# Softmax probabilities of a streaming encoder's cross-attention as fp16 halves, turned round by a DMA transpose instead of by TensorE

## The reference, cut to what matters

```
q = x_q.reshape(b, t, MEM_HEADS, MEM_HEAD_DIM)                       # 4 heads of 64
s = jnp.einsum('bthd,bmhd->bhtm', q, mem_k).astype(jnp.float32) * (MEM_HEAD_DIM ** -0.5)
p = jax.nn.softmax(s, axis=-1).astype(mem_v.dtype)                   # over 256 memory tokens
o = jnp.einsum('bhtm,bmhd->bthd', p, mem_v).reshape(b, t, GROUP_W)
y_x = o * jax.nn.silu(x_g)
```

## Time and profile before

| | us |
|---|---|
| three timed runs | 1544.96, 1550.85, 1550.87 (median 1550.85) |
| profiled execution, own time | 1546.23 |
| its span, first to last instruction | 1544.4 |
| busy: PE / DVE / ACT / POOL | 1482.1 / 1122.6 / 533.2 / 241.4 |
| mean granted TensorE clock | 0.986 |

### The profile page before, as it was taken

The page is one execution under the profiler, slowest core; times in us unless marked ns, Lnnn a source line. Parts: engine busy times, 40 slices in busy tenths (PEclk is TensorE's granted clock), DMA queues, the critical chain, the costliest instruction groups (busy, mean ns, idle before and its releaser), DMA issues.

```text
span 1544.4 us, 32608 instructions
## 1 busy us (share of the span) xinstructions
PE 1482.1 (96%) x12014; PEld 1291.5 (84%) x12014; DVE 1122.6 (73%) x3012; ACT 533.2 (35%) x1093; POOL 241.4 (16%) x188
## 2 busy tenths in 40 slices
PE   5877999999999999999999999999999999999976
PEld 4766888888888898888888888888889888888864
DVE  7996675949587685949677694958767694958754
ACT  7773232332233332323323232323323233233332
POOL 2252110111111111111111011111110011111100
PEclk9988999999999999999999999999999999999988
DMA  9884607154442706354451615354260625444136
GB/s 270 237 300 131 225 18 231 79 163 163 163 163 61 251 28 193 120 163 163 131 195 34 236 58 178 146 163 163 93 233 14 216 97 163 163 150 171 43 113 239
DMA packets 148771, 236.19 MB, mean 153 GB/s; under 512 B 71945, under 2 KB 97725, under 8 KB 148733
## 3 DMA queue, kind: packets, MB, share of 16 engines
q1 hardware_dynamic: 148733, 235.69, 45.4%
HBM read 193.62 MB, written 26.05 MB: 142 GB/s over the span
## 4 chain that ended last, share of the span: by engine, by line
PE 86%; DVE 8%; DMA 2%; ACT 1%; issue 1%; SPq 1%; DVEq 0%; ACTq 0%
PE u L431 19%; PE u L432 19%; PE u L433 19%; PE sps L431 4%; PE sps L433 4%; PE sps L432 4%; PE qps L431 3%; PE qps L433 3%; PE qps L432 3%; DVE z L1177 3%; PE qps L507 2%; DVE w_hl L1159 2%; PE ops L431 1%; PE ops L432 1%; PE ops L433 1%
## 5 line engine op out<-in xcount | busy, mean ns | idle before, releaser
L431 PE MATMUL u<-h_hi,w_hl 128*128 128x256 f16 (+1 forms) x2992 | 789.6, 270 | 4.5 <-issue 1.9
L432 PE MATMUL u<-h_lo,w_hl 128*128 128x256 f16 (+1 forms) x2992 | 788.7, 269 | 0.0
L433 PE MATMUL u<-h_hi,w_hl 128*128 128x256 f16 (+1 forms) x2992 | 788.6, 269 | 0.0
L1177 DVE SCALAR_TENSOR_TENSOR z<-glu,cst,z 128x256 f32<-128x256 f32 (+1 forms) x1020 | 432.8, 494 | 0.5
L431 PEld LDWEIGHTS u<-h_hi,w_hl 128*128 128x128 f16 x2992 | 293.8, 99 | 47.8 <-issue 7.9
L433 PEld LDWEIGHTS u<-h_hi,w_hl 128*128 128x128 f16 x2992 | 293.6, 99 | 32.6
L432 PEld LDWEIGHTS u<-h_lo,w_hl 128*128 128x128 f16 x2992 | 293.7, 99 | 31.4
L734 ACT ACTIVATE gate<-u,inv 128x256 f32<-128x256 f32 (+1 forms) x204 | 83.7, 462 | 244.4 <-PE u L433 242.6
L1517 DVE TENSOR_TENSOR ob<-sps,ob 128x512 f32<-128x512 f32 (+1 forms) x33 | 21.3, 686 | 132.8 <-PE sps L433 132.8
L431 PE MATMUL sps<-ring,y_hi 128*128 128x512 f32 (+1 forms) x280 | 111.6, 398 | 3.2 <-DVE y_lo L1214 2.5
L431 PE MATMUL qps<-ring,y_hi 128*128 128x512 f32 (+1 forms) x264 | 106.2, 402 | 8.3 <-DMA ring<-wo_split 8.3
(11 more groups left out here) (195 smaller groups left out, 2011.0 us busy)
## 6 DMA issues: line engine op xcount, KB each, us to landing
ring<-wo_split SPq DMA_DIRECT2D x264, 512.0 KB, 6.5
ob<-in_x_prompt SPq DMA_DIRECT2D x34, 512.0 KB, 3.7
out<-ob SPq DMA_DIRECT2D x32, 512.0 KB, 3.1
xb<-in_x_prompt SPq DMA_DIRECT2D x30, 512.0 KB, 4.9
w_hl<-in_w_in SPq DMA_DIRECT2D x20, 512.0 KB, 7.4
wo_split<-ring SPq DMA_DIRECT2D x16, 512.0 KB, 3.9
rows<-in_w_out SPq DMA_DIRECT2D x16, 256.0 KB, 4.9
ob<-in_mem_prompt SPq DMA_DIRECT2D x2, 512.0 KB, 6.5
```

Of the source, the lines that this page charges most:

```text
L431: nc.tensor.matmul(out, a_hi, b_hi, start=first, stop=False)
L432: nc.tensor.matmul(out, a_hi, b_lo, start=False, stop=False)
L433: return nc.tensor.matmul(out, a_lo, b_hi, start=False, stop=last)
L1177: ins = nc.vector.scalar_tensor_tensor(z[:, c, 0:n], glu[:, c, k:k + n], w, z[:, c, 0:n], ALU.mult, ALU.add)
```

## The change

- The probabilities of a pair are no longer transposed on PE. ACT writes the high half straight from `probs`, multiplied by the reciprocal, as fp16 into the row-major buffer `prow`; DVE writes the remainder (`probs_lo`: probs times reciprocal minus the high half). `softmax_norm` shrinks to `softmax_rcp`, two small instructions; the probabilities carry a factor of 2^14.
- SP then issues one DMA transpose of both tiles and both halves of the pair (`probs_across`, 128 x 2048 fp16), behind ring piece 6 (pair 0) and piece 7 (pair 1), whose loads move from the chunk's start to this place.
- `prow` is one buffer for both pairs, so `probs_hi` of a pair waits until the transpose of the pair before has landed.
- The values become fp16 halves with one scale for all, a power of two from their sum of squares (`value_squares` on ACT, `value_sum` on PE, `value_scale` on DVE); `yx_out` multiplies by the inverse. `attend` is still 12 matmuls of 256 columns with 128-column stationaries, in fp16.
- The second tile of the next rows goes into `xp`, the memory of `probs`, not into `xb`. In chunk 0 the wait for `row_lo` moves from before the ninth ring piece to behind the sixteenth.
- The cached values and keys for the sample are loaded earlier, into `probs`, and their handling has other places in the lists.

```
-            sp.dma_start ... xb[:, :], x_next  (q == RING - 1, after the wait for row_lo)
@@ SP, sync_chunk
                 if first:
+                    for p in range(PAIRS):
+                        sp.wait_ge(p_lo_ok.sem, (p + 1) * nt)
+                        probs_across(p, n)
+                    sp.dma_start(xp, x_next).then_inc(x_in[1].sem, 16)
                     sp.wait_ge(wlo_ok.sem, FT)
...
-                        sp.wait_ge(o_piece.sem, o_piece.at(i, q - RING + 1))
+                        if not first and RING - PAIRS <= q < RING:
+                            sp.wait_ge(p_lo_ok.sem, p_lo_ok.at(i, (q - RING + PAIRS + 1) * nt))
+                        else:
+                            sp.wait_ge(o_piece.sem, o_piece.at(i, q - RING + 1))
                         sp.dma_start(ring[:, q % RING].bitcast(F32), wo_split[q]).then_inc(wo_in[q % RING].sem, 16)
+                        if not first and RING - PAIRS <= q < RING:
+                            probs_across(q - RING + PAIRS, n)
...
-                    if q == RING and rows_m:
-                        if x_next is None:
+                    if q == (PIECES - 1 if first else RING) and rows_m:
+                        if first or x_next is None:
                             sp.wait_ge(row_lo_ok.sem, row_lo_ok.at(i, 1))
                         row_across(0, rows_m[0])
@@ PE, attend
-                        ins = three(ops[:, p * N:p * N + n], v_hi[:, k, p, v], v_lo[:, k, p, v],
-                                    pt_hi[:, h, k, 0:n], pt_lo[:, h, k, 0:n], ...
+                pe.wait_ge(pt_in[p].sem, pt_in[p].at(i, 16))
+                products = [(va, pa, k, h) for h in range(2) for k in range(MT) for va, pa in ((0, 0), (0, 1), (1, 0))]
+                for step, (va, pa, k, h) in enumerate(products):
+                    ins = nc.tensor.matmul(ops[:, p * N:p * N + n].rearrange("d (t m) -> d t m", t=nt),
+                                           v16[:, va, k, p, h * HD:h * HD + P], pt16[:, p, 0:nt, pa, h, k, 0:m], ...
@@ ACT, probs_hi
+                act.wait_ge(rcp_ok.sem, rcp_ok.at(i, 2 * p + 2))
+                if n == N and needed(pt_in[1 - p].at(i, 16 * p)):
+                    act.wait_ge(pt_in[1 - p].sem, pt_in[1 - p].at(i, 16 * p))
+                for t, t0, m in tiles(n):
+                    for h in range(2):
+                        ins = nc.scalar.activation(prow[0:m, s % 2, 0, h, :], probs[0:m, s % 2, h, :], ACT.Copy,
+                                                   scale=rcp[0:m, s, h:h + 1])
@@ DVE, probs_lo
+                        ins = nc.vector.scalar_tensor_tensor(prow[0:m, s % 2, 1, h, :], probs[0:m, s % 2, h, :],
+                                                             rcp[0:m, s, h:h + 1], prow[0:m, s % 2, 0, h, :],
+                                                             ALU.mult, ALU.subtract)
@@ PE, chunk
                 project(i, n, "a_x")
-                probs_t(i, n, 0)
                 scores(i, n, 1)
                 project(i, n, "a_b")
                 attend(i, n, 0)
                 project(i, n, "a_g")
-                probs_t(i, n, 1)
                 mix(i, n)
                 project(i, n, "b_g")
                 attend(i, n, 1)
@@ DVE, chunk
-                softmax_norm(i, n, 0)
+                softmax_rcp(i, n, 0)
-                taps(i, n, 12, 15)
+                taps(i, n, 12, 14)
+                probs_lo(i, n, 0)
+                taps(i, n, 14, 15)
```

More of the change, by code:

```diff
@@ L493, in scores @@
                 ins.then_inc(s_ready.sem, 1)
[L495 to L509, removed]
             def attend(i, n, p):
@@ L516, in attend, with value_sum @@
                         pe.wait_ge(v_l.sem, 1)
[L517 to L520, removed]
[L521 to L524 removed]
+                    if type(i) is int and i == CHUNKS:
+                        pe.wait_ge(v_l.sem, 2)
+                pe.wait_ge(pt_in[p].sem, pt_in[p].at(i, 16))
+                nt, m = len(tiles(n)), min(n, P)
+                products = [(va, pa, k, h) for h in range(2) for k in range(MT) for va, pa in ((0, 0), (0, 1), (1, 0))]
+                for step, (va, pa, k, h) in enumerate(products):
+                    ins = nc.tensor.matmul(ops[:, p * N:p * N + n].rearrange("d (t m) -> d t m", t=nt),
+                                           v16[:, va, k, p, h * HD:h * HD + P], pt16[:, p, 0:nt, pa, h, k, 0:m],
+                                           start=step == 0, stop=step == len(products) - 1)
+                ins.then_inc(pv_ready.sem, 1)
+            def value_sum(k):
+                pe.wait_ge(vsq_ok.sem, k + 1)
+                if k == 0:
+                    pe.wait_ge(mn_lo.sem, 4)
+                    bank = qps[:, 0, 0:2]
+                else:
+                    pe.wait_ge(yx_ok.sem, yx_ok.at(LAST, 1))
+                    bank = ops[:, 0:2]
+                nc.tensor.matmul(bank, ones[:, :], tiny[:, :], start=True, stop=False)
+                nc.tensor.matmul(bank, ones[:, :], V_SQ[k], start=False, stop=True).then_inc(vsum_ok.sem, 1)
             def constants():
@@ L570, in out_project @@
                 pe.wait_ge(exp_ok.sem, exp_ok.at(i, 4 if n == N else 2))
-                pe.wait_ge(pt_lo_ok.sem, pt_lo_ok.at(i, 4))
+                if type(i) is int and i == 0:
+                    pe.wait_ge(vscl_ok.sem, 1)
+                else:
+                    pe.wait_ge(r_ok.sem, r_ok.at(i, 0))
                 for q in range(PIECES):
@@ L737, in squares @@
             def squares(j, t, m, i=0, rows=xb, loaded=None):
-                act.wait_ge(loaded or x_in.sem, 16 if loaded else 16 * (j - 3))
+                if loaded:
+                    act.wait_ge(loaded, 16)
+                else:
+                    act.wait_ge(x_in[t].sem, x_in[t].at(i, 16))
                 if needed(j):
@@ L999, in first_chunk @@
                 d_high(0, N)
+                probs_hi(0, N, 0)
                 piece_hi(12)
@@ L1019, in first_chunk @@
                 row_hi(0, *nxt[0])
-                squares(*nxt[1])
+                squares(*nxt[1], rows=xp)
                 z_silu(0, N)
```

195 lines of the change are left out of this document (111 added, 84 removed).

## The result

| | before | after |
|---|---|---|
| timed runs, median | 1550.43 (1544.96 to 1550.87, 4 runs) | 1540.24 (1539.66 to 1541.21, 4 runs) |
| profiled execution, own time / span | 1546.23 / 1544.4 | 1541.21 / 1539.4 |

Ratio 0.9943, 95% interval 0.992 to 0.9966: faster by 0.6% where 1.3% was forecast. The time lies inside the stated range of 1511 to 1549; of the 20 us that were forecast 10.2 came.

A forecast was written before the change was run, and what follows sets the result against it. TensorE was taken as the bound in the 15 chunks after chunk 0. 1546.2 - 15 (loop) - 10.5 (chunk 0) + 8 (end) = 1528.7, with half the median's offset 1531 us; range 1511 to 1549.

The forecast's parts named there:

- three signs of being wrong: PE waits for `pt` in the loop, `b_g` waits for nothing, or the sample's attend doesn't wait for the DMA.
- rival 2: Loop: DVE late, remainders cost 0.1 more each, the loop gains nothing but 0.1; 1544 us with the median's offset; chance 0.15.
- Chunk 0: Output projection of chunk 0: the stall goes as ring reloads wait only for their slots; -10.5 us, bounds -12 and -4.
- it has idle time to regain it by 100: Chunk 0: ACT stands still 6 us near 78 us for the values' scale, and regains that delay by 100.
- Rival 4: Chunk 0 gains little because ACT's stop at 78 us is not regained: 1537 us; chance 0.08.
- The loop: 15 chunks after chunk 0: `b_g` starts 0.87 us earlier, attend of pair 1 gives 0.12; 15 x 1.0 = -15 us.
- PE's 1.94: Loop: TensorE work saved per chunk, 0.90 and 0.8 from transposes, 0.12 from each attend, if nothing else is late.
- `ab_out` stays where it was, to within 0.3: DVE in the loop: 4.3 us removed, 4.4 added, so `ab_out` stays at 824.43 to 825.30 in chunk 8.
- Rival 1: Loop: PE gets all of the gain, `b_g` isn't held up, 15 x 1.94 = 29; about 1515 us; chance 0.2.
- The DMA path: Loop: transposes land 5.7 us after first issue, with slack of 1.9 for pair 0, 1.7 for pair 1; no cost.
- switch of 0.1: PE in the loop: `mix` alone is 6 matmuls at 0.118 and a switch of 0.1, about 0.8 us.
- The end: Values' chain +1; sample chunk stalls 11 us behind seven ring pieces, 4 given back; +8 us, bounds +2 and +12.

The follow-up runs named there:

- p5: Changed kernel with plain copies for DMA transposes, chunk 0's wait for `row_lo` put back ahead of the ninth ring piece: span 1545.7 us.
- p2: Changed kernel with plain copies for DMA transposes, `value_scale` earlier on DVE in chunk 0: span 1535.7 us.
- p9: Changed kernel with plain copies, `value_scale` early in chunk 0, `ab_out` ahead of pair 1's remainders, pair 1's attend behind `c_g`: span 1515.7 us.
- p1: Changed kernel with plain copies; in the loop `d_high` ahead of pair 1's `probs_hi`, `d_low` and `ab_out` ahead of its remainders: 1537.92 us, ratio 0.993.
- p0_after: Changed kernel with its DMA transposes made plain copies of as many bytes, the base for experiments on it: median 1539.93 us, ratio 0.9942.
- p3: p1 with one more edit, pair 1's attend behind the projection of `c_g` on PE: 1519.07 us, ratio 0.9816.
- p0_before: Kernel before the change with the DMA transposes of `row_across` made plain copies of as many bytes: median 1545.73 us, ratio 0.999.
- p4: Changed kernel with plain copies, the sample's first eight ring pieces issued behind chunk 15's state stores, probability copies ahead of the `ob` load: span 1528.9 us.
- p6: Changed kernel with plain copies, three ring pieces instead of one directly ahead of pair 0's copies in each chunk after the first: span 1562.2 us.

## Why the prediction was wrong

Of the 12.5 us between the sum (1528.7) and the execution's own time (1541.2), 6.3 are chunk 0, 4.8 the loop, 1.4 the end. None of the prediction's three signs of being wrong came: the waits stand where it put them, and two terms were too large. That the time lies within 4 us of rival 2's 1544 is luck: there the loop gains 2 us, here 10.2.

1. **Chunk 0, -10.5 forecast, -4.2 measured.** "Lost: 9.8" was right: 44.68 became 34.91, and p5 takes back 7.4 of it by the wait alone. What failed is the sentence on ACT's stop, "it has idle time to regain it by 100", and with it "landing at 118". The stop, 4.9 us where 6 stood, was not regained, and the landing came at about 122.5. `b_gate` and `z_stats` both came 5.6 later. ACT's rows ahead of `b_gate`, before, then after:

```profile
116.42 2.19 ACT L784 ACTIVATE w_hl<-ob,w_scl 128x1024 f16<-128x1024 f32 x2 [0.90 <-DVE w_scl L1148]
...
119.92 0.84 ACT L734 ACTIVATE gate<-u,inv 128x256 f32<-128x256 f32 x2
```

```profile
119.14 2.19 ACT L812 ACTIVATE w_hl<-ob,w_scl 128x1024 f16<-128x1024 f32 x2 [1.08 <-DVE w_scl L1187]
122.48 1.71 ACT L858 ACTIVATE prow<-probs,st 128x256 f16<-128x256 f32 x4 [1.15 <-issue]
```

   The last two `w_high` come 2.7 later, for DVE's `w_scl`; about 2.5 is what the stop was worth (p2, p9). Then 1.15 of idle, where the code waits for pair 0's landing, and 1.7 for pair 1's high halves, which now stand ahead of `b_gate`. Together 5.6; the sum had the last two at nothing.

   Behind `b_gate` the clock adds to it. The stretch from `b_gate` to `z_stats` before, after, and in p1:

```profile
119.92:129.16 9.24, 8.61 (x76) 7.63 (x75) 8.43 (x17) 5.30 (x12) 3.36 (x2) 1.00 0.31 113
```

```profile
125.50:134.73 9.23, 8.34 (x60) 7.09 (x61) 4.42 (x13) 3.55 (x9) 2.83 (x2) 0.82 0.79 227
```

```profile
125.76:133.34 7.58, 6.69 (x60) 6.09 (x61) 4.95 (x13) 3.53 (x9) 3.73 (x2) 1.00 0.74 203
```

   It takes 7.58 to 7.60 in all nine runs p1 to p9, at 1.00; 9.23 in the changed kernel at 0.82, and 10.53 in p0_after at 0.68. Before, it took as long as in the changed kernel for another reason: PE had 76 matmuls left there and not 60. So of the 5.6 us by which `z_stats` is late, 1.6 is the lower clock behind `b_gate`; at full clock 3.9 would be left. Granted clock in three earlier stretches, before, then after:

```profile
100.00:110.00 10.00, 9.63 (x92) 8.32 (x89) 10.00 (x14) 7.65 (x13) 8.96 (x6) 1.00 0.93 337
110.00:120.00 10.00, 6.47 (x55) 5.47 (x56) 9.97 (x20) 9.04 (x18) 1.27 (x1) 1.00 0.40 163
120.00:130.00 10.00, 9.37 (x82) 8.39 (x81) 9.11 (x18) 5.37 (x12) 3.91 (x3) 1.00 0.29 107
```

```profile
100.00:110.00 10.00, 5.02 (x34) 3.76 (x32) 10.00 (x13) 8.65 (x16) 7.54 (x5) 0.83 0.99 371
110.00:120.00 10.00, 7.04 (x41) 5.25 (x40) 9.46 (x16) 7.59 (x16) 5.09 (x3) 0.66 0.81 296
120.00:130.00 10.00, 7.57 (x53) 5.93 (x52) 8.90 (x18) 7.34 (x14) 0.56 (x1) 0.84 0.61 123
```

   PE stood 5.0 us until 106.9 for DVE's `w_low(17)` and then ran in part at the lower level, where before it ran at full clock. Rival 4 was the stop's part of this, at 0.08.

2. **The loop, -15 forecast, -10.2 measured.** The mechanism was right: `b_g` waits for `ab_out`, and all of PE's 1.94 is there to be had (2.03 in p3). The term was mis-sized twice. "`ab_out` stays where it was, to within 0.3" became +0.4, so `b_g` gained 0.55 and not 0.87. DVE's own sum was good: from the end of the taps ahead of the first pair's reciprocals to the end of `ab_out` it takes 19.4 where 19.5 stood. The other 0.5 was lost just ahead of them, where the scaling of `xb` and two taps meet POOL (2.13 for the scaling, 1.28 before). The new lists needn't be its cause: in p0_before, with the old ones, the scaling takes 2.13 as well.

   `mix`, "0.2, inside the wait for `b_g`", waited 0.40. And the two stops cost 0.4 a chunk beside their idle time, which the sum had at nothing. Together 2.03 - 0.95 - 0.4 is the 0.7 of chunk 8 (87.80 to 87.08). Rival 1 is thereby refuted for this order of DVE; rival 2 was right only in that `ab_out` came late.
3. **The DMA path** was right: 5.3 to landing where 5.7 stood, no wait in the loop, and a slack (1.7 in the text, 1.6 with plain copies in p1) of the size forecast.
4. **The 0.09 that PE gave beyond the 1.94** is the prediction's "switch of 0.1" at `mix`. In p3 `b_g` starts 0.82 behind the last matmul of `a_g` (803.02, 803.84): one slot of 0.11 and six matmuls in 0.71, no switch. Before it was 1.70 (824.62, 826.32), so 0.88 went and not 0.8. The attends gave the 0.12 each of the sum: from the last matmul ahead of one to the first behind it 1.54 before (817.94, 819.48), 1.42 after (808.50, 809.92).
5. **The end, +8 forecast, +9.4 measured.** The queue of ring pieces was the cause (p4). The transpose landed at 1506.0, 9.7 us after its issue, where "9 us at this rate" had stood. From the output projection's end to the sample's `glu_out` it takes 10.8 us instead of 9.3: the values' chain is +1.5 where +1 stood.

## What to carry to other kernels

When a bound engine is relieved, list every wait that then lies within the gain: here `d_low`, `ab_out` and the landing of pair 1 stood within 2 us of each other; taking two away and moving the third (p1) gave 0.24 us a chunk, clearing all three 1.36. A DMA put into a latency chain belongs ahead of bulk loads in the queue, above all at a boundary where they all become free at once (20.8 us of waiting or 7.6). An engine's stop in a start-up phase isn't regained just because the engine has idle time later: ask which engine it waits for then, and what stands behind it.

## What the runs showed of the hardware

- The granted clock punishes a short stop unevenly: of 13 stops of 1.8 to 2.6 us in p6 seven were followed by the lower clock and six were not. Of three of 2.06 us, those that end at 641.26 and 818.93 were, that at 730.92 was not. Six kernels with the same chunk 0 up to `z_stats` (p0_after, p1, p3 to p6) reached it between 132.6 and 136.2. In 130 to 135 us the slowest of them, p0_after, had a granted clock of 0.72 and p3 1.00.
- DVE and POOL (GpSimd) hold each other up, whole instructions at a time. Before, DVE's scaling of `xb` started at 802.60 and took 1.28 us, POOL's addition started at 802.58 and took 2.24. After, the same DVE instruction took 2.13 (794.05) and POOL's 1.08 (794.02). The Trainium skill, "SBUF — State Buffer", section "SBUF: two separate sides", says that the port pair the two share is an exclusive lock, held for the whole instruction by whichever comes first. These pairs agree with it: one instruction takes its own time, the other about both together (2.24 and 2.13, against 1.28 + 1.08), and the loser changed. Which came first the starts don't tell: POOL's is the earlier by 0.02 or 0.03 in both.
- A DMA transpose of 512 KB within SBUF occupied SP's issue for 3.4 us, and four plain copies of the same bytes for 2.7.
